# Twelve gate products ahead of every step of the grouped heads' attention, latent heads first, and one instruction less per row in the norms

## The chip, the cores and the metric

One core of a Trainium2 chip runs the whole kernel. The time is the device time of one launch, in microseconds (us). The engines are named as in the profile: PE (TensorE, matmuls; PEld its weight loads), DVE (VectorE), ACT (ScalarE), POOL (GpSimd) and SP, which issues the DMAs. Each has its own queue and works through it in order; they wait for one another through semaphores.

## The reference

Two transformer layers over 512 tokens of width 1024, then a second block with four more token mixers. The change touches the mixer of the two layers and all norms:

```
for l in range(2):
    x = x + 0.5 * g1 * swiglu(modulate(x, sh1, sc1), ...)
    x = x + g2 * token_mix(modulate(x, sh2, sc2), ...)
    x = x + 0.5 * g3 * swiglu(modulate(x, sh3, sc3), ...)

modulate(x, shift, scale) = rms_norm(x) * (1 + scale) + shift

token_mix(u):
    o_a = nsa_attention(...)   # grouped heads: 8 heads in 2 groups; compressed, selected and window branch
    o_b = mla_attention(...)   # latent heads: 8 heads, key width 64 + 32
    y = sigmoid(g_a) * (o_a @ w_branch_a) + sigmoid(g_b) * (o_b @ w_branch_b)
    return y @ w_out
```

`g_a` and `g_b` are `u` times the last 2048 columns of `w_in`: 16 groups of 128 columns. Softmax is masked and causal. With 512 tokens all blocks are selected, so the selected branch is a causal attention over all keys, like the window branch. Everything is fp32.

## The kernel before, in words

**Matmuls of weights.** Activations lie feature-major in SBUF, as 128 x 512 tiles `u[:, k, :]`. Each weight tile arrives by DMA in `raw` (512 KB for 8 blocks of 128 x 128), ACT rounds it to `wh` (L917), DVE writes the rest to `wl` (L1393). The activation is split in the same way into `uh` and `ul`. A block of k is then three products, `wh*uh`, `wl*uh`, `wh*ul` (helper `three`, L435 to L437), each with 512 columns. A list (`plan`) gives the order of the weight tiles. Every engine walks it with `get`, which prepares the tile two ahead.

**Norms.** DVE multiplies a row of x by the reciprocal root, which PE has spread into a PSUM bank (L1457). ACT scales and shifts the row (L951), ACT rounds it to `uh` (L953), DVE subtracts to get `ul` (L1427). The next matmul waits for the first `ul`. The order of the four is in `apply`, on ACT and on DVE.

**Attention of a layer** (`mix`, stages `m0` and `m1`). It is a software pipeline over 48 steps, each a pair of heads and one block i of 128 queries against 128(i+1) keys. 32 steps are grouped heads (kind `nsa`: 4 pairs, i from 0 to 3, two branches), then 16 latent heads (kind `mla`: 4 pairs, i from 0 to 3). A step t goes through

```
PE    scores(t)                        L638, two heads, banks 2*(t%2) and 2*(t%2)+1
DVE   add bias, row minimum (t)        L1660, 'soft' of both heads
ACT   exp (t)                          L1085
DVE   max, reciprocal, scale (t)       L1668, L1670, L1676 or L1678
PE    transpose (t)                    L544, 'turning', banks 4 and 5
ACT   copy (t)                         L1092
PE    values (t)                       L651, L657, banks 6 and 7
```

In each round of the loop PE issues scores(t), turning(t-2), values(t-3), in this order. DVE issues soft(t), then the scaling of t-1:

```
for t in range(len(pairs) + 1):        # DVE
    if t < len(pairs):  ... soft(t)
    if t > 0:           ... max, reciprocal, scale of t - 1
```

The grouped heads' soft needs `slope`, which POOL makes from the table `dist` (L2130) once the latent projections are done. The latent heads' soft needs the table `mask`.

**After the attention** come, for each m of 8, the gate group gA (24 products), the branch product wa (12), gB (24) and wb (12), L435 to L437; ACT takes the gate's tanh (L1110), DVE makes the sigmoid (L1691), the product with the branch (L1694), the sum (L1696) and the split `yh`, `yl`. Then eight groups `wo` read `yh`, `yl`.

Of the kernel before, what the change touches and what calls it, by code (L numbers as in the profile page):

```python
# [14 lines left out]
def plan():  # L15
# [42 lines left out]
    for l in range(2):  # L58
# [22 lines left out]
        for m in range(8):  # L81
            fm(f"gA{l}", 8, m)
            fm(f"wa{l}", 4, m)
            fm(f"gB{l}", 8, m)
            fm(f"wb{l}", 4, m)
# [141 lines left out]
def attention_pairs():  # L227


    u = [("nsa", hh, i, br) for hh in range(4) for i in range(4) for br in range(2)]  # L230
    return u + [("mla", j, i, 0) for j in range(4) for i in range(4)]


def program(nc, A, OUT):
# [42 lines left out]
    with ExitStack() as c:  # L277
        oA, oB = sb(c, "oA", [128, 4, 512]), sb(c, "oB", [128, 4, 512])
        with ExitStack() as c1:
# [6 lines left out]
            dist = sb(c1, "dist", [128, 512])  # L286
            mq = sb(c1, "mq", [128, 8, 512])
            mk = sb(c1, "mk", [128, 8, 512])
# [4 lines left out]
            with ExitStack() as c2:  # L293
                mmask = sb(c2, "mmask", [128, 512])
# [6 lines left out]
        yh, yl = sb(c, "yh", [128, 8, 512], F32R), sb(c, "yl", [128, 8, 512], F32R)  # L301
# [44 lines left out]

    ident, ones = col("ident", 0, 128), col("ones", 0, 128)
# [55 lines left out]
    def tensor_engine(pe, TE):  # L403
# [143 lines left out]
        def mix(l):  # L547
# [71 lines left out]
            pe.wait_ge(*s_act["kk", st])  # L619
            pe.wait_ge(*s_act["vt", st])  # L620
            pe.wait_ge(*s_act["pcT", st])
            for t in range(len(pairs) + 3):
                if t < len(pairs):
                    kind, h, i, br = pairs[t]
                    L = 128 * i + 128
                    if t == 32:
                        pe.wait_ge(*s_act["mk", st])
                        pe.wait_ge(*s_dve["mk", st])
                        pe.wait_ge(*s_dve["mq", st])
                        pe.wait_ge(*s_pool["mq", st])  # L630
                        pe.wait_ge(*s_act["mv", st])
                    o = [take(("S", (st, 2 * t + g)), 2 * (t % 2) + g) for g in range(2)]
                    for g in range(2):
                        if kind == "nsa":
                            q, k = oA[64 * g:64 * g + 64, h, sl(i)], kk[64 * g:64 * g + 64, br, 0:L]
                        else:
                            q, k = mq[0:96, 2 * h + g, sl(i)], mk[0:96, 2 * h + g, 0:L]
                        TE.matmul(o[g][:, 0:L], q, k, start=True, stop=True).then_inc(*s_pe.up(("ps", ("S", (st, 2 * t + g)))))  # L638
# [3 lines left out]
                if 0 <= t - 3 < len(pairs):  # L642
# [9 lines left out]
                    for j in range(i + 1):  # L652
                        for g in range(2):
# [4 lines left out]
                            if j == i:  # L658
                                last = g == 1 and i == 3 and (kind == "mla" or br == 1)
                                ins.then_inc(*s_pe.up(("pv", (st, n + g)), *([("ps", both)] if last else [])))  # L660
            s_pe.mark(("attend", st))
            ring[1] = 0
            for m in range(8):
                for x_, h_, l_ in (("A", oAh, oAl), ("B", oBh, oBl)):
                    fm(("g" + x_, st, m), f"g{x_}{l}", 8, m, uh, ul, ("u", st))
# [237 lines left out]
    def scalar_engine(act, SC):  # L903
# [41 lines left out]
        def apply(st, n, dst, scale, shift=None, before_k=None):  # L945
            for k in range(n):
                if before_k:
                    before_k(k)
                t0 = tmp[k % 4]
                act.wait_ge(*s_dve["ap", st, k])  # L950
                SC.activation(t0[:], t0[:], ACT.Identity, bias=0.0 if shift is None else shift(k), scale=scale(k)).then_inc(*s_act.up(("af", st, k)))  # L951
                act.wait_ge(*s_act.now())
                SC.activation(dst[:, k, :], t0[:], ACT.Copy).then_inc(*s_act.up(("uh", st, k)))  # L953
# [6 lines left out]
        def norm(st):  # L960
            q = MOD[st]
            apply(st, 8, uh, lambda k: mod[:, q + 8 + k:q + 9 + k], lambda k: mod[:, q + k:q + k + 1])
# [57 lines left out]
        def mix(l):  # L1020
# [38 lines left out]
            apply(("cq", st), 3, qh, lambda k: col(f"qn{l}", k))  # L1059
# [3 lines left out]
            for h in range(8):  # L1063
                fm(f"uq{l}", 3, h)
                copy(("uq", st, h), mq[0:64, h, :], bank(("uq", st, h))[0:64, :], ("mq", st, h), -(96.0 ** -0.5))
                if h == 4:
                    apply(("ckv", st), 2, ch, lambda k: col(f"kvn{l}", k))
# [10 lines left out]

            for t in range(len(pairs) + 3):
                if 0 <= t - 1 < len(pairs):  # L1080
                    L = 128 * pairs[t - 1][2] + 128
                    for n in (2 * t - 2, 2 * t - 1):
                        p = mP[n % 6]
                        act.wait_ge(*s_dve["s", (st, n)])
                        SC.activation(p[:, 0:L], p[:, 0:L], ACT.Exp, bias=two(n, 0), scale=-1.0, accum_out=two(n, 1)).then_inc(*s_act.up(("e", (st, n))))  # L1085
                if 0 <= t - 2 < len(pairs):
                    L = 128 * pairs[t - 2][2] + 128
                    for n in (2 * t - 4, 2 * t - 3):
# [3 lines left out]
                        SC.activation(mT[n % 4][:, 0:L], bank(("T", (st, n)))[:, 0:L], ACT.Copy).then_inc(*s_act.up(("pt", (st, n)), frees=("T", (st, n))))  # L1092
                if 0 <= t - 3 < len(pairs):
# [6 lines left out]
            for k in range(4):  # L1100
                for kind, o, h in (("nsa", oA, oAh), ("mla", oB, oBh)):
                    act.wait_ge(*s_act["o", st, kind, k])
                    SC.activation(h[:, k, :], o[:, k, :], ACT.Copy).then_inc(*s_act.up(("oh", st, kind, k)))
            for m in range(8):
                for b, (x_, w_) in enumerate((("gA", "wa"), ("gB", "wb"))):
                    fm(f"{x_}{l}", 8, m)
                    act.wait_ge(*s_pe["ps", (x_, st, m)])
                    if m > 1:
                        act.wait_ge(*s_dve["y", st, m - 2])
                    SC.activation(tmp[(2 * m + b) % 4][:], bank((x_, st, m))[:], ACT.Tanh, scale=0.5).then_inc(*s_act.up((x_, st, m), frees=(x_, st, m)))  # L1110
                    fm(f"{w_}{l}", 4, m)
                act.wait_ge(*s_dve["ysum", st, m])
                SC.activation(yh[:, m, :], tmp[2 * m % 4][:], ACT.Copy).then_inc(*s_act.up(("yh", st, m)))
# [250 lines left out]
        apply("f10", 8, uh, lambda k: mod[:, q0 + 8 + k:q0 + 9 + k], lambda k: mod[:, q0 + k:q0 + k + 1], rest)  # L1364
# [9 lines left out]
        apply("s", 8, uh, lambda k: small[:, 64 + k:65 + k])  # L1374
        copy(("r1",), acc[:], bank(("r1",))[:], "rowcopy")
        second()
        apply("up", 8, uh, lambda k: col("n2", k))
# [3 lines left out]
    def vector_engine(dve, V):  # L1381
# [67 lines left out]
        def apply(st, key, src, n, g, dst_h, dst_l, before_k=None, after_k=None):  # L1449
            for k in range(n + 1):  # L1450
                if k < n:
# [5 lines left out]
                    V.tensor_tensor(tmp[k % 4][:], src[:, k, :], more[:] if after_k and k else bank(g)[:], MUL).then_inc(  # L1457
                        *s_dve.up(("ap", st, k), frees=g if k == (0 if after_k else n - 1) else None))
                    if after_k:
                        after_k(k)  # L1460
                        low(dst_l[:, k, :], tmp[k % 4][:], dst_h[:, k, :], s_act["uh", st, k], (*key, k))
                elif after_k:
                    continue
                if k > 0 and not after_k:
                    low(dst_l[:, k - 1, :], tmp[(k - 1) % 4][:], dst_h[:, k - 1, :], s_act["uh", st, k - 1], (*key, k - 1))
# [61 lines left out]
        def mix(l):  # L1527
# [75 lines left out]
            apply(("cq", st), ("cq", st), cq, 3, ("rq", st), qh, ql)  # L1603
# [22 lines left out]
            for h in range(8):  # L1626
# [4 lines left out]
                if h == 4:  # L1631
                    dve.wait_ge(*s_dve["added", st, 4])
                    apply(("ckv", st), ("ckv", st), ckv, 2, ("rk", st), ch, cl)
# [7 lines left out]
            dve.wait_ge(*table(f"dist {st}"))  # L1641

            for t in range(len(pairs) + 1):
                if t < len(pairs):
# [37 lines left out]
            for k in range(4):  # L1682
                low(oAl[:, k, :], oA[:, k, :], oAh[:, k, :], s_act["oh", st, "nsa", k], ("oA", st, k))
# [747 lines left out]
```

## Time and profile before

| | |
|---|---|
| time, median of 3 runs | 3555.81 us (3555.67 to 3568.52) |
| time of the profiled execution | 3571.1 us |
| its span, first to last instruction | 3569.3 us |
| PE busy | 3455.7 us, 97% |
| DVE busy | 1800.9 us, 50% |
| ACT busy | 1237.3 us, 35% |
| mean granted TensorE clock | 0.975 of full speed |
| chain that ended last | PE 89%, DVE 6%, ACT 3% |

PE's matmuls are pipelined, and their ends are modelled: a 128x512 product is shown with 0.39 us, while the next one starts 0.23 us after it. For the cost of PE work, starts are to be read, not durations. An idle time shown in brackets is what is left after the modelled end.

### The profile page before, as it was taken

The page shows a single profiled execution, that of the slowest core. Times are in us where ns is not written, and L with a number is a line of the kernel's source. Part 1 is how long each engine was busy: PE and PEld are TensorE (multiplying, and loading weights), DVE is VectorE, ACT ScalarE, POOL GpSimd, SP SyncE. Part 2 cuts the span into 40 slices and gives each one's busy share as a digit, 9 for nine tenths or more (in the row PEclk, how much of TensorE's full clock was granted, in tenths as well). Part 3 has the DMA queues.
Part 4 walks back from the last instruction along what each step waited for, and adds up shares of the span by engine and source line. Part 5 has one row for each costly group of instructions (what it writes and reads, how often), then busy time and mean ns, then how long its engine had stood idle before and what let it go on. Part 6 is the DMA issues. An engine that isn't in the chain of part 4 may idle for free.

```text
span 3569.3 us, 40894 instructions
## 1 busy us (share of the span) xinstructions
PE 3455.7 (97%) x16646; PEld 2777.9 (78%) x16646; DVE 1800.9 (50%) x3132; ACT 1237.3 (35%) x2064; POOL 286.5 (8%) x238
## 2 busy tenths in 40 slices
PE   8999999999999999999899999999999999999999
PEld 6888776787888788877667878887778777878887
DVE  7666457645566733334674443334453665354433
ACT  4222337523222322223573232224322444124322
POOL 0000121002000200021200100012011000020000
PEclk9999999999999999999899999999999999899999
DMA  6565221133565533232102322322221223132332
GB/s 235 207 210 185 99 79 37 40 106 101 190 219 195 175 97 102 92 101 92 59 1 83 103 83 85 111 81 93 66 77 61 76 68 117 31 100 81 98 106 77
DMA packets 120217, 376.36 MB, mean 105 GB/s; under 512 B 13280, under 2 KB 28000, under 8 KB 120032
## 3 DMA queue, kind: packets, MB, share of 16 engines
q1 hardware_dynamic: 120032, 373.76, 32.2%
q8 instruction: 132, 2.16, 0.3%
q14 instruction: 53, 0.43, 0.0%
HBM read 371.61 MB, written 2.10 MB: 105 GB/s over the span
## 4 chain that ended last, share of the span: by engine, by line
PE 89%; DVE 6%; ACT 3%; issue 1%; POOL 1%; DMA 0%; SPq 0%; POOLq 0%; ACTq 0%; DVEq 0%
PE ps L435 25%; PE ps L436 25%; PE ps L437 25%; PE ps L638 2%; PE ps L544 2%; PE ps L657 1%; PE ps L478 1%; PE ps L485 1%; PE ps L469 1%; PE ps L471 1%; PE ps L470 1%; DVE s_wl L1393 1%; ACT s_wh L917 0%; ACT s_tmp L951 0%; POOL s_small L2061 0%
## 5 line engine op out<-in xcount | busy, mean ns | idle before, releaser
L1393 DVE TENSOR_TENSOR s_wl<-s_raw,s_wh 128x1024 fp32r<-128x1024 f32 (+3 forms) x645 | 708.3, 1100 | 867.3 <-ACT s_wh L917 865.2
L435 PE MATMUL ps<-s_uh,s_wh 128*128 128x512 f32 x2696 | 1075.1, 399 | 36.9 <-DVE s_ul L1427 23.9
L436 PE MATMUL ps<-s_uh,s_wl 128*128 128x512 f32 x2696 | 1060.0, 393 | 0.0
L437 PE MATMUL ps<-s_ul,s_wh 128*128 128x512 f32 x2696 | 1059.6, 393 | 0.0
L917 ACT ACTIVATE s_wh<-s_raw 128x1024 fp32r<-128x1024 f32 (+3 forms) x645 | 588.2, 913 | 742.1 <-PE ps L437 555.3
L435 PEld LDWEIGHTS ps<-s_uh,s_wh 128*128 128x128 f32 x2696 | 513.2, 190 | 155.5 <-issue 31.8
L436 PEld LDWEIGHTS ps<-s_uh,s_wl 128*128 128x128 f32 x2696 | 513.4, 190 | 107.9 <-issue 2.7
L437 PEld LDWEIGHTS ps<-s_ul,s_wh 128*128 128x128 f32 x2696 | 512.0, 190 | 108.7
L437 PE MATMUL ps<-s_fl,s_wh 128*128 128x512 f32 x960 | 378.2, 394 | 0.0
L435 PE MATMUL ps<-s_fh,s_wh 128*128 128x512 f32 x960 | 378.2, 394 | 0.0
L436 PE MATMUL ps<-s_fh,s_wl 128*128 128x512 f32 x960 | 378.2, 394 | 0.0
L984 ACT ACTIVATE s_fh<-s_tmp 128x512 fp32r<-128x512 f32 x120 | 75.8, 632 | 407.2 <-DVE s_tmp L1490 382.3
L436 PEld LDWEIGHTS ps<-s_fh,s_wl 128*128 128x128 f32 x960 | 179.5, 187 | 44.5
L437 PEld LDWEIGHTS ps<-s_fl,s_wh 128*128 128x128 f32 x960 | 179.5, 187 | 44.5
L435 PEld LDWEIGHTS ps<-s_fh,s_wh 128*128 128x128 f32 x960 | 179.5, 187 | 44.3
L978 ACT ACTIVATE s_tmp<-ps 128x512 f32<-128x512 f32 x120 | 71.7, 597 | 345.6 <-PE ps L437 343.2
L1402 DVE CUSTOM_DVE_ANT_0 s_raw<-s_raw,s_crow 128x1024 f32<-128x1024 f32 x144 | 181.3, 1259 | 0.8 <-DMA s_raw<-w 0.8
L2067 POOL TENSOR_TENSOR s_acc<-s_x 128x512 f32<-128x512 f32 x7 | 8.8, 1259 | 1776.4 <-DVE s_x L1472 1714.0
L1490 DVE TENSOR_TENSOR s_tmp<-s_tmp,ps 128x512 f32<-128x512 f32 x88 | 60.4, 687 | 171.7 <-PE ps L437 169.9
L1427 DVE TENSOR_TENSOR s_fl<-s_tmp,s_fh 128x512 fp32r<-128x512 f32 x120 | 83.1, 692 | 83.8 <-ACT s_fh L984 83.8
L1472 DVE SCALAR_TENSOR_TENSOR s_x<-ps,s_mod,s_x 128x512 f32<-128x512 f32 x80 | 60.0, 750 | 111.0 <-PE ps L437 111.0
L2072 POOL TENSOR_TENSOR s_acc<-s_acc,s_tmp 128x512 f32<-128x512 f32 x42 | 83.2, 1982 | 3.3
(405 smaller groups left out, 3673.4 us busy)
## 6 DMA issues: line engine op xcount, KB each, us to landing
s_raw<-w SPq DMA_DIRECT2D x616, 512.0 KB, 3.6
s_raw<-w SPq DMA_DIRECT2D x96, 192.0 KB, 2.4
s_raw<-w SPq DMA_DIRECT2D x64, 256.0 KB, 2.6
s_raw<-w SPq DMA_DIRECT2D x19, 128.0 KB, 2.1
s_x<-x SPq DMA_DIRECT2D x4, 512.0 KB, 6.2
out<-s_x SPq DMA_DIRECT2D x8, 256.0 KB, 2.2
s_raw<-w SPq DMA_DIRECT2D x4, 420.0 KB, 4.0
s_crow<-crow SPq DMA_DIRECT2D x2, 512.0 KB, 3.4
```

The source lines that it names most:

```text
L435: TE.matmul(o, w_hi(i, k), h, start=first, stop=False)
L436: TE.matmul(o, w_lo(i, k), h, start=False, stop=False)
L437: return TE.matmul(o, w_hi(i, k), l, start=False, stop=last)
L544: ins = TE.transpose(o[:, sl(j)], p[:, sl(j)], ident)
L638: TE.matmul(o[g][:, 0:L], q, k, start=True, stop=True).then_inc(*s_pe.up(("ps", ("S", (st, 2 * t + g)))))
L917: SC.activation(wh[slot[t]][:, 0:n], raw[t % NRAW][:, 0:n], ACT.Copy).then_inc(*s_hi.up(("hi", t)))
L978: SC.activation(s[:], bank(("g", st, jj))[:], ACT.Silu if u else ACT.Relu).then_inc(*s_act.up(("gate", st, jj), frees=("g", st, jj)))
L984: SC.activation(fh[:, j, :], s[:], ACT.Copy).then_inc(*s_act.up(("hh", st, jj)))
L1393: V.tensor_tensor(wl[w][:, 0:n], raw[t % NRAW][:, 0:n], wh[w][:, 0:n].bitcast(F32), SUB).then_inc(*s_lo.up(("lo", t)))
L1402: V.tensor_tensor_reduce(raw[i % NRAW][:], raw[i % NRAW][:], crow[:], 1.0, 0.0, MUL, ADD, mod[:, o:o + 1]).then_inc(*s_dve.up(("raw", i)))
L1427: V.tensor_tensor(dst, src, hi.bitcast(F32), SUB).then_inc(*s_dve.up(key))
L2072: PO.tensor_tensor(acc[:], acc[:], t[:], ADD).then_inc(*s_pool.up(("sq", st, m), ("sq", st)))
```

## The change

- The latent heads' 16 steps come first, the grouped heads' 32 after them.
- Of the 16 gate groups of a layer, 15 move into the grouped heads' steps: from the first of them (step 16) on, every step begins on PE with two quarters of a group, twelve products in one piece, for 30 steps. The groups use banks 2 and 3, and the grouped heads' scores only banks 0 and 1. The last group stands between the attention and wa.
- In all 48 steps PE now issues turning(t-2), values(t-3), and scores(t) last; before, scores(t) stood first. DVE's order is as it was.
- The tables `dist` and `mask` change places: `mask` is loaded early, `dist` once the latent projections are done.
- Gate tanhs go to `sA`, `sB` (the latent heads' `mq`, `mk`, by then read); `yh`, `yl` are now `uh`, `ul`. The sigmoid's scaling is folded into other instructions.
- Norms: DVE multiplies by the spread root and the scale in one instruction, ACT adds the shift and rounds in one, DVE adds the shift and subtracts in one: three instead of four.
- POOL clears its tiles in the mixer only when the norm is through.

```diff
 def attention_pairs():
-    u = [("nsa", hh, i, br) for hh in range(4) for i in range(4) for br in range(2)]
-    return u + [("mla", j, i, 0) for j in range(4) for i in range(4)]
+    u = [("mla", j, i, 0) for j in range(4) for i in range(4)]
+    return u + [("nsa", hh, i, br) for hh in range(4) for i in range(4) for br in range(2)]
+FIRST_NSA = 16
+FILLED = 15
+def gate_pieces(t):
+    return [(n // 4, n % 4) for n in (2 * (t - FIRST_NSA), 2 * (t - FIRST_NSA) + 1) if 0 <= n < 4 * FILLED]
...
+            def piece(n, quarter):
+                m, x_ = n // 2, "AB"[n % 2]
+                g = ("g" + x_, st, m)
+                if quarter == 0:
+                    gate_now["mix"] = get(f"g{x_}{l}", 0, 128 * m), take(g, 2 + n % 2)
+                i, o = gate_now["mix"]
+                for k in (2 * quarter, 2 * quarter + 1):
+                    ins = three(o[:, :], i, k, uh[:, k, :], ul[:, k, :], k == 0, k == 7)
...
             for t in range(len(pairs) + 3):
-                if t < len(pairs):
-                    ... scores(t)
+                for n in gate_pieces(t):
+                    piece(*n)
                 if 0 <= t - 2 < len(pairs):
                     for n in (2 * t - 4, 2 * t - 3):
                         turn((st, n), 4 + n % 2, mP[n % 6], 128 * pairs[t - 2][2] + 128)
                 if 0 <= t - 3 < len(pairs):
                     ... values(t - 3)
+                if t < len(pairs):
+                    ... scores(t)
             s_pe.mark(("attend", st))
+            for quarter in range(4):
+                piece(15, quarter)
...
-                SC.activation(t0[:], t0[:], ACT.Identity, bias=0.0 if shift is None else shift(k), scale=scale(k))
-                SC.activation(dst[:, k, :], t0[:], ACT.Copy)
+                if shift is None:
+                    SC.activation(dst[:, k, :], tmp[k % 4][:], ACT.Copy)
+                else:
+                    SC.activation(dst[:, k, :], tmp[k % 4][:], ACT.Identity, bias=shift(k), scale=1.0)
...
-                    V.tensor_tensor(tmp[k % 4][:], src[:, k, :], more[:] if after_k and k else bank(g)[:], MUL)
+                    V.scalar_tensor_tensor(tmp[k % 4][:], src[:, k, :], scale(k), more[:] if after_k and k else bank(g)[:], MUL, MUL)
...
+                    V.scalar_tensor_tensor(dst_l[:, k, :], tmp[k % 4][:], shift(k), dst_h[:, k, :].bitcast(F32), ADD, SUB)
```

**Where the latent heads' steps change.** PE's queue in the latent heads of layer 0, before; `s_mk,s_mq` are scores, `s_cst,s_mP` or `s_cst,s_tmp` turning, `s_mT,s_mv` values:

```order
L638 MATMUL ps2<-s_mk,s_mq 128x512
L638 MATMUL ps3<-s_mk,s_mq 128x512
L544 MATMUL ps4<-s_cst,s_mP2 128x128 x2
L544 MATMUL ps5<-s_cst,s_mP3 128x128 x2
L657 MATMUL ps7<-s_mT0,s_mv 64x128
L657 MATMUL ps7<-s_mT1,s_mv 64x128
L638 MATMUL ps0<-s_mk,s_mq 128x128
L638 MATMUL ps1<-s_mk,s_mq 128x128
L544 MATMUL ps4<-s_cst,s_tmp0 128x128 x3
L544 MATMUL ps5<-s_cst,s_tmp1 128x128 x3
```

and the same place with the change:

```order
L684 MATMUL ps0<-s_mk,s_mq 128x384
L684 MATMUL ps1<-s_mk,s_mq 128x384
L554 MATMUL ps4<-s_cst,s_tmp0 128x128 x2
L554 MATMUL ps5<-s_cst,s_tmp1 128x128 x2
L661 MATMUL ps7<-s_mT0,s_mv 64x128
L661 MATMUL ps7<-s_mT1,s_mv 64x128
L684 MATMUL ps2<-s_mk,s_mq 128x512
L684 MATMUL ps3<-s_mk,s_mq 128x512
L554 MATMUL ps4<-s_cst,s_mP0 128x128 x3
L554 MATMUL ps5<-s_cst,s_mP1 128x128 x3
```

The turning that followed scores(512 keys) turned two blocks, those of the step two before it; now it turns three blocks, those of the step just before the 512-key step. Between scores(t-1) and turning(t-2) there stood turning(t-3), values(t-4) and scores(t), and now nothing stands there.

**What DVE does between the two.** DVE's queue in the same steps with the change (`ISA` with `s_mmask` is the soft of one head, `s_mfew` alone its accumulator):

```order
L1707 ISA s_mP0,s_mfew<-ps2,s_mmask 128x512
L1707 ISA s_mfew 128x1
L1707 ISA s_mP1,s_mfew<-ps3,s_mmask 128x512
L1707 ISA s_mfew 128x1
L1715 TENSOR_SCALAR s_mfew<-s_mfew 128x2
L1717 RECIPROCAL s_mfew<-s_mfew 128x2
L1725 TENSOR_SCALAR s_tmp0<-s_tmp0,s_mfew 128x384
L1725 TENSOR_SCALAR s_tmp1<-s_tmp1,s_mfew 128x384
```

The scaling of the 384-key step, which its turning waits for, stands behind the soft of the 512-key step, which waits for that step's scores. This order is that of before.

**Where the grouped heads' steps change.** PE's queue in a step of the grouped heads with the change (`s_uh,s_wh` and so on are gate products, `s_kk,s_oA` scores, `s_mT,s_vt` values):

```order
L446 MATMUL ps2<-s_uh,s_wl0 128x512
L447 MATMUL ps2<-s_ul,s_wh0 128x512
L554 MATMUL ps4<-s_cst,s_mP0 128x128 x2
L554 MATMUL ps5<-s_cst,s_mP1 128x128 x2
L661 MATMUL ps6<-s_mT2,s_vt 64x128
L661 MATMUL ps6<-s_acc,s_vt 64x128
L684 MATMUL ps0<-s_kk,s_oA 128x384
L684 MATMUL ps1<-s_kk,s_oA 128x384
L445 MATMUL ps2<-s_uh,s_wh0 128x512
L446 MATMUL ps2<-s_uh,s_wl0 128x512
```

Here twelve gate products stand between scores(t-1) and turning(t-2), of which the first two and the last two are shown.

## Rows read from the trace of the kernel before

**Rows 1.** Busy time by stretch: PE, PEld, DVE, ACT, POOL, then clock, DMA, GB/s.

```profile
548.26:672.02 123.76, 117.38 (x977) 76.08 (x976) 94.00 (x384) 93.50 (x296) 12.22 (x8) 0.97 0.01 4
672.02:804.34 132.32, 132.32 (x578) 108.09 (x578) 60.80 (x84) 43.55 (x64) 0.00 (x0) 1.00 0.31 98
1759.10:1882.51 123.41, 116.94 (x972) 75.96 (x972) 94.06 (x384) 92.97 (x295) 11.68 (x8) 0.97 0.01 4
2770.00:2790.00 20.00, 16.72 (x79) 12.46 (x78) 13.84 (x50) 8.83 (x25) 0.00 (x0) 1.00 0.10 28
```

**Rows 2.** Timeline (start us, us, engine, line, op), the attention's first steps, layer 0.

```profile
549.01 0.49 PE L638 MATMUL ps<-s_kk,s_oA 64*128 64x128 f32 x4 [0.26 <-ACT s_mv L943]
550.11 0.29 DVE L1660 CUSTOM_DVE_ANT_0 s_mP<-ps,s_slope 128x128 f32<-128x128 f32 x1 [4.82 <-POOL s_slope L2130]
...
552.03 0.80 PE L638 MATMUL ps<-s_kk,s_oA 64*128 64x256 f32 x2 [2.52 <-DVE s_mfew L1660]
```

**Rows 3.** Timeline, four latent steps of layer 0, PE and DVE.

```profile
642.95 1.98 PE L638 MATMUL ps<-s_mk,s_mq 96*128 96x512 f32 x4
...
644.77 0.60 PE L544 MATMUL ps<-s_cst,s_mP 128*128 128x128 f32 x4
644.97 0.69 DVE L1660 CUSTOM_DVE_ANT_0 s_mP<-ps,s_mmask 128x512 f32<-128x512 f32 x1 [0.16 <-PE ps L638]
...
645.59 0.16 DVE L1668 TENSOR_SCALAR s_mfew<-s_mfew 128x2 f32<-128x2 f32 x1
...
645.99 0.75 DVE L1678 TENSOR_SCALAR s_tmp<-s_tmp,s_mfew 128x384 f32<-128x384 f32 x2
...
648.88 1.04 PE L544 MATMUL ps<-s_cst,s_mP 128*128 128x128 f32 x8
...
649.84 0.48 DVE L1678 TENSOR_SCALAR s_mP<-s_mP,s_mfew 128x128 f32<-128x128 f32 x2
...
653.39 0.70 PE L638 MATMUL ps<-s_mk,s_mq 96*128 96x512 f32 x1
```

**Rows 4.** Timeline, grouped heads, a turning that waits for its scaling.

```profile
596.13 0.73 DVE L1676 TENSOR_SCALAR s_mP<-s_mP,s_mfew,s_gt 128x256 f32<-128x256 f32 x2
...
596.69 0.41 PE L544 MATMUL ps<-s_cst,s_mP 128*128 128x128 f32 x2 [0.21 <-DVE s_mP L1676]
```

**Rows 5.** Timeline of PE, a piece of six gate products in the second block.

```profile
2777.70 0.50 PE L435 MATMUL ps<-s_uh,s_wh 128*128 128x512 f32 x1 [1.65 <-ACT s_sg L1143]
...
2779.20 0.59 PE L538 MATMUL ps<-s_xqk 128*128 128x256 f32 x2
```

**Rows 6.** Groups by line and shape: xcount | busy us, mean ns | idle before.

```profile
L917 ACT ACTIVATE s_wh<-s_raw 128x1024 fp32r<-128x1024 f32 x463 | 486.5, 1052 | 416.6 <-PE ps L437 258.2 <-DMA s_raw<-w 97.2 <-PE ps L471 60.3
L1393 DVE TENSOR_TENSOR s_wl<-s_raw,s_wh 128x1024 fp32r<-128x1024 f32 x463 | 596.4, 1290 | 573.6 <-ACT s_wh L917 573.3
L1472 DVE SCALAR_TENSOR_TENSOR s_x<-ps,s_mod,s_x 128x512 f32<-128x512 f32 x80 | 60.0, 750 | 111.0 <-PE ps L437 111.0
```

**Rows 7.** Timeline of PE, fifteen products that read uh, ul, and fifteen with yh, yl.

```profile
411.31 0.39 PE L435 MATMUL ps<-s_uh,s_wh 128*128 128x512 f32 x1
...
414.71 0.39 PE L435 MATMUL ps<-s_uh,s_wh 128*128 128x512 f32 x1
...
805.04 0.39 PE L435 MATMUL ps<-s_yh,s_wh 128*128 128x512 f32 x1
...
808.54 0.39 PE L435 MATMUL ps<-s_yh,s_wh 128*128 128x512 f32 x1
```

**Rows 8.** Timeline, first row of the norm ahead of the mixer, layer 0.

```profile
400.13 0.63 ACT L953 ACTIVATE s_uh<-s_tmp 128x512 fp32r<-128x512 f32 x1
...
400.79 0.69 DVE L1427 TENSOR_TENSOR s_ul<-s_tmp,s_uh 128x512 fp32r<-128x512 f32 x1 [1.03 <-ACT s_uh L953]
...
401.63 0.77 PE L435 MATMUL ps<-s_uh,s_wh 128*128 128x512 f32 x1 [3.19 <-DVE s_ul L1427]
```

More of the change, by code:

```diff
@@ L82, in plan @@
             fm(f"gA{l}", 8, m)
+            fm(f"gB{l}", 8, m)
+        for m in range(8):
             fm(f"wa{l}", 4, m)
-            fm(f"gB{l}", 8, m)
             fm(f"wb{l}", 4, m)
@@ L617, in mix @@
             s_pe.mark(("latent", st))
-            pe.wait_ge(*s_act["kk", st])
-            pe.wait_ge(*s_act["vt", st])
-            pe.wait_ge(*s_act["pcT", st])
-            for t in range(len(pairs) + 3):
-                if t < len(pairs):
[L624 to L638, printed above, removed]
+            def piece(n, quarter):
[6 more added lines that the diff above has]
+                    ins = three(o[:, :], i, k, uh[:, k, :], ul[:, k, :], k == 0, k == 7)
+                if quarter == 3:
+                    ins.then_inc(*s_pe.up(("w", i), ("ps", g)))
+            for t in range(len(pairs) + 3):
+                for n in gate_pieces(t):
+                    piece(*n)
                 if 0 <= t - 2 < len(pairs):
@@ L1077, in mix, with gate @@
             act.wait_ge(*s_pe["latent", st])
+            def gate(n):
+                m, x_ = n // 2, "AB"[n % 2]
+                act.wait_ge(*s_pe["ps", ("g" + x_, st, m)])
+                SC.activation((sA if n % 2 == 0 else sB)[:, m, :], bank(("g" + x_, st, m))[:], ACT.Tanh, scale=0.5).then_inc(
+                    *s_act.up(("g" + x_, st, m), frees=("g" + x_, st, m)))
             for t in range(len(pairs) + 3):
@@ L1085, in mix @@
                         SC.activation(p[:, 0:L], p[:, 0:L], ACT.Exp, bias=two(n, 0), scale=-1.0, accum_out=two(n, 1)).then_inc(*s_act.up(("e", (st, n))))
+                for n, quarter in gate_pieces(t):
+                    if quarter == 0:
+                        get(f"g{'AB'[n % 2]}{l}", 0, 128 * (n // 2))
                 if 0 <= t - 2 < len(pairs):
@@ L1092, in mix @@
                         SC.activation(mT[n % 4][:, 0:L], bank(("T", (st, n)))[:, 0:L], ACT.Copy).then_inc(*s_act.up(("pt", (st, n)), frees=("T", (st, n))))
+                for n, quarter in gate_pieces(t - 1):
+                    if quarter == 3:
+                        gate(n)
                 if 0 <= t - 3 < len(pairs):
@@ L1099, in mix @@
             act.wait_ge(*s_dve["attend", st])
-            for k in range(4):
-                for kind, o, h in (("nsa", oA, oAh), ("mla", oB, oBh)):
+            get(f"gB{l}", 0, 128 * 7)
+            for kind, o, h in (("nsa", oA, oAh), ("mla", oB, oBh)):
+                for k in range(4):
                     act.wait_ge(*s_act["o", st, kind, k])
                     SC.activation(h[:, k, :], o[:, k, :], ACT.Copy).then_inc(*s_act.up(("oh", st, kind, k)))
+            gate(15)
             for m in range(8):
[L1105 to L1111, printed above, removed]
+                fm(f"wa{l}", 4, m)
+                fm(f"wb{l}", 4, m)
                 act.wait_ge(*s_dve["ysum", st, m])
-                SC.activation(yh[:, m, :], tmp[2 * m % 4][:], ACT.Copy).then_inc(*s_act.up(("yh", st, m)))
+                SC.activation(yh[:, m, :], sA[:, m, :], ACT.Copy, scale=0.5).then_inc(*s_act.up(("yh", st, m)))
             for m in range(8):
@@ L1456, in apply @@
                         dve.wait_ge(*s_act["row", st])
-                    V.tensor_tensor(tmp[k % 4][:], src[:, k, :], more[:] if after_k and k else bank(g)[:], MUL).then_inc(
+                    V.scalar_tensor_tensor(tmp[k % 4][:], src[:, k, :], scale(k), more[:] if after_k and k else bank(g)[:], MUL, MUL).then_inc(
                         *s_dve.up(("ap", st, k), frees=g if k == (0 if after_k else n - 1) else None))
@@ L1640, in mix @@
             dve.wait_ge(*s_pe["latent", st])
-            dve.wait_ge(*table(f"dist {st}"))
             for t in range(len(pairs) + 1):
+                for n, quarter in gate_pieces(t):
+                    if quarter == 0:
+                        get(f"g{'AB'[n % 2]}{l}", 0, 128 * (n // 2))
                 if t < len(pairs):
@@ L2220, in sync_engine @@
             sp.wait_ge(*s_pe["latent", st])
-            tab(f"mask {st}", mmask[:], A["mask"])
+            tab(f"dist {st}", dist[:], A["dist"])
             if l == 0:
```

105 lines of the change are left out of this document (65 added, 40 removed).

## Prediction

> **What bounds the kernel now.** I read the stretches first, then the timeline inside them. In both layers' attention PE is busy 117 of 124 us, and in the gates and branches behind it 132.32 of 132.32 [rows 1]. DVE and ACT have 94 us each in an attention of 48 steps, under 2.0 us a step, while a step takes 2.6 us. So PE is the bound, and only two things can change the time: what PE waits for, and what a product costs it. Moving 15 gate groups saves no product. The most it can save is PE's waits in the attention: 123.76 less 117.38 is 6.4 us, and a clock of 0.97 means that some 3% of the stretch, 3.5 us, was lost at 1.2 GHz [rows 1]. That is 10 us a layer. As a record's modelled end hides a part of each gap, I take 12, and 10 to 14 as bounds. Where these are: at the start the first soft waits 4.82 us for POOL's slope, and PE then 2.52 us for a bank, and there the clock fell [rows 2]; the rest is spread in fractions of a microsecond. The gates' own stretch has nothing to save.
>
> **The new order, latent heads: the main term.** Turning(t-2) needs the scaling of t-2. On DVE that stands behind soft(t-1), which needs scores(t-1). Before, PE had turning(t-3), values(t-4) and scores(t) between scores(t-1) and turning(t-2), one whole step, 10.44 / 4 = 2.6 us from 642.95 to 653.39 [rows 3]. Now scores stand last in a round, and the latent steps have no piece at their head: nothing is between. PE stands still from the moment it could issue turning until DVE has gone through soft, max, reciprocal and one head's scaling. The length of that can be read off. With 512 keys PE is free at 644.77; DVE starts the second head's soft at 644.97, max at 645.59, scaling at 645.99, so 1.22 us after [rows 3]. From the start of a scaling to the turning that waits for it is 0.56 us [rows 4]. Together 1.8 us. For 256 keys the scaling starts 649.84 - 648.88 = 0.96 us after; its heads have 128 keys, 0.24 instead of 0.37 us each, so 0.43 behind it: 1.4 us [rows 3, 4]. The mean is 1.6 us. It is paid in steps 2 to 15, 14 times: 22.4 us a layer. Bounds: below, 1.0 us a step (if the transpose's start overlaps part of it), 14 us; above 2.0, 28 us. The exp, which the scaling needs too, was issued a step earlier and is long done.
>
> **The start.** The latent heads need no slope, so the 4.82 us wait of DVE goes and `dist` and POOL's work hide behind 16 steps. But their scores need all four copies of the latent values: the second pair of scores before had to wait for such a copy until 549.01 [rows 2], and the first had started at 548.26 [rows 1]. So the start slips by 0.8 us.
>
> **The grouped heads: pieces.** Twelve products stand ahead of every turning. A piece of six took 2779.20 - 2777.70 = 1.50 us [rows 5]. At the bare rate, fifteen in 3.40 us or 0.227 each [rows 7], six are 1.36, so a piece costs 0.14 us on top to get in and out of. Twelve: 2.72 + 0.14 = 2.86 us. 30 pieces: 4.2 us more than the same products in a row. What they give: the chain from scores to turning is, with the two heads' scores ending together and so both softs in series (0.6 more), at most 2.4 us, and the piece of 2.86 covers it; so the small waits there go (they are in the 12). What the pieces bring for the others is, in every second step, one 1024-wide rounding on ACT (1052 ns) and one rest on DVE (1290 ns) [rows 6], and a tanh: 2.8 us a step for ACT and 2.6 for DVE, where PE now takes 2.86 + 2.2 = 5.1. The weights are asked for more slowly than in the gates' stretch, where the DMA share was 0.31 [rows 1].
>
> **The end.** Two grouped steps, and the turning behind the last scores, have no piece: the bare chain three times, 2.0 to 2.4 us, 6.6; the drain of the last two turnings and values some 1.3, as before. 7.9 us. The last gate group covers the way from the last values to wa.
>
> **Sum of a layer:** 22.4 + 0.8 + 4.2 + 7.9 = 35.3 us of new waits and switches, less the 12 of before: +23.3. Two layers: +46.6 us. The split and sigmoid work behind has 5.6 us of PE per m and no new wait.
>
> **wo.** Fifteen products on `yh`, `yl` took 3.50 us, on `uh`, `ul` 3.40 [rows 7]. If that is due to where the tiles lie, the 384 products of wo gain 0.0067 us each, 2.6 us; if it is not, nothing. I take 2.
>
> **Norms.** The first row's chain goes straight to PE: the wait for the first `ul` is 3.19 us [rows 8]. The subtraction could start when the second ACT instruction does now: 400.79 - 400.13 = 0.66 us sooner. Its two DVE instructions with a scalar take 750 ns [rows 6] instead of 0.69, 0.12 lost: 0.53 net, eight norms, 4.2 us. The inner norms of the mixer (cq, ckv) are partly covered; I take 1 us a layer. Together 6; bounds 2 and 10.
>
> **Clock.** The old start's fall goes with its wait (it is in the 12). The new latent steps leave PE still for 1.6 of each 4.2 us. In 2770 to 2790 PE stood still for 3.3 of 20 us, once for 1.65 at a stretch, and the clock stayed at 2.4 GHz [rows 1, 5]; at the attention's start it fell to 1.2 after 2.52 us [rows 2]. The new waits lie between, nearer to the first. I expect a fall now and then, +3 us in all. All latent steps at 1.2 GHz is a rival.
>
> The Trainium skill, "TensorE: Matmul & The Clock Gate", Part 4: PE-mode transpose, says that transposes don't count as busy for the clock as other matmuls do. By that rule the latent steps, a quarter of which are transposes, would look idler than their records, and the first rival below would be the forecast. The trace of before does not bear it out: its attention has as many transposes and after the start keeps the full clock, though there with hardly a wait beside them.
>
> **Total:** +46.6 - 2 - 6 + 3 = +42 us on the profiled execution's 3571.1: 3613. That execution stands 15.3 us over the median of the three runs, 3555.8, which I take to be luck unconnected with the change. So the forecast for the median is **3598 us**, 1.2% slower. A measurement of this kernel can tell about 0.5%, 18 us, from no change.
>
> **Rivals.**
> - *Clock low through the latent heads.* For it: waits in every one of 14 steps. Against: the full clock in 2770 to 2790. About three quarters of the 10.44 us per four steps is columns, which double: +7.8, four times, +31 us a layer if it is low all the time, so 3598 + 62 = 3660; low half the time 3629. Chance 0.16.
> - *The filled steps are not PE's.* ACT's rounding stands behind its exps, DVE's rest behind that, and the next soft behind the rest: soft 1.3, exps 1.4, rounding 1.05, rest 1.3 add up to 5.0 us, as long as PE's 5.1. Should POOL's slopes or a late weight stretch it, each of 15 new tiles holds PE up by some 0.5 us: +15 in both layers, 3613. Chance 0.10.
> - *Not slower.* It decides from the point at which DVE has the scaling of t-2 done before scores(t-1) ends, so that PE finds it ready in the latent steps. Against: DVE's order has the soft first, before and now. For: only that the trace of before hardly shows the wait, as a step covered it. Then the 22.4 and most of the 6.6 are gone: 35.3 - 22.4 - 5 = 8 against 12, so -4 a layer, -8 in both, -2 - 6 for wo and norms: 3540. Chance 0.12.
> - The forecast's own case: 0.62.
>
> **How the numbers follow.** In its own case the sum moves with the wait per step (14 to 28 us a layer around 22.4, so -17 to +11 for both), the 12 (4 down), the norms and wo (4 either way) and the clock (up to 10): 3575 to 3625. To hold 8 in 10 the range takes in the second rival and half of the first: 3572 to 3642. Faster by over 0.5% is a part of the last rival, 0.04; within 0.5% the rest of it and the lower edge of my own case, 0.09; slower 0.87.
>
> **What would show it.** In the latent steps of the changed kernel, the first transposes of each step with an idle time of 1 to 1.5 us (the modelled end hides some) put down to DVE's scaling L1725, and a step of 4.2 us instead of 2.6. The grouped steps at 5.0 to 5.2 us with next to no idle time. A stretch from the first scores to the end of the last gate group of some 234 us at full clock. No wait of DVE for the slope. wo's products at 0.227. The norm's first product 0.5 us sooner. I am wrong if the latent steps stay under 3 us, or if idle time appears ahead of the gate products.

## The result, and the profile after

| | before | changed |
|---|---|---|
| time, median of 4 launches each | 3559.7 us (3555.7 to 3568.5) | 3631.2 us (3616.6 to 3643.0) |
| ratio | | 1.0193, 95% interval 1.0172 to 1.0214 |
| profiled execution | 3571.1 us | 3616.6 us, span 3614.7 us |
| PE busy | 3455.7 us | 3467.0 us, 96% |

The change makes the kernel 1.9% slower. The forecast was 3598 us, in 3572 to 3642. The table has four launches of before, one more than the table ahead of the prediction. The profiled execution is the fastest of the changed kernel's four, 3616.6 us with a mean granted clock of 0.973; the others, 3624.9, 3637.5 and 3643.0 us, had 0.970, 0.965 and 0.963. The four of before stand within 13 us of each other, these within 26.

The stretches of the changed kernel, from its trace (columns as in [rows 1]): latent heads of layer 0, grouped heads of layer 0 with their pieces, latent heads of layer 1, and in layer 0 the last gate group with the branch products.

```profile
543.88:614.14 70.26, 50.79 (x254) 30.51 (x255) 28.16 (x118) 31.08 (x92) 5.97 (x4) 0.77 0.02 5
614.14:786.06 171.92, 165.27 (x1084) 120.54 (x1083) 84.94 (x281) 90.33 (x234) 6.15 (x4) 0.97 0.12 38
1784.49:1850.11 65.62, 46.04 (x253) 27.47 (x254) 28.10 (x117) 30.84 (x91) 5.96 (x4) 0.84 0.02 6
786.06:836.12 50.06, 50.06 (x216) 40.25 (x216) 34.97 (x54) 20.28 (x34) 0.00 (x0) 1.00 0.36 105
```

Before, the grouped and the latent steps of layer 0, each from their first scores to their last:

```profile
548.26:621.82 73.56, 68.82 (x586) 42.14 (x586) 59.11 (x243) 56.68 (x183) 12.22 (x8) 0.95 0.02 5
624.17:665.23 41.06, 40.55 (x312) 28.20 (x311) 29.23 (x123) 30.22 (x97) 0.00 (x0) 1.00 0.00 1
```

The sixteen latent steps are where the time went. Before, they took 41 us. Now they take 70 and 66 us, PE is idle for 19.5 of each, and the clock is at 0.77 and 0.84 of full speed, so half of the first stretch and a third of the second ran at 1.2 GHz. In the stretch of the pieces PE is busy for 165.27 of 171.92 us; the 6.7 us in which it waits are ahead of the three turnings that have no piece, 2.0 to 2.4 us each.

The same place as [rows 3], four latent steps at full clock, PE and then DVE, start us, us, engine, line, operation, and in brackets the idle time:

```profile
568.58 1.56 PE L684 MATMUL ps<-s_mk,s_mq 96*128 96x384 f32 x4
571.55 0.68 PE L554 MATMUL ps<-s_cst,s_tmp 128*128 128x128 f32 x4 [1.42 <-ACT s_mP L1116]
572.16 0.44 PE L661 MATMUL ps<-s_mT,s_mv 128*64 128x128 f32 x4
572.53 1.98 PE L684 MATMUL ps<-s_mk,s_mq 96*128 96x512 f32 x4
576.13 0.85 PE L554 MATMUL ps<-s_cst,s_mP 128*128 128x128 f32 x6 [1.62 <-ACT s_mP L1116]
...
577.50 0.71 PE L684 MATMUL ps<-s_mk,s_mq 96*128 96x128 f32 x4
579.50 1.07 PE L554 MATMUL ps<-s_cst,s_mP 128*128 128x128 f32 x8 [1.28 <-DVE s_mP L1725]
...
581.30 1.13 PE L684 MATMUL ps<-s_mk,s_mq 96*128 96x256 f32 x4
583.65 0.50 PE L554 MATMUL ps<-s_cst,s_tmp 128*128 128x128 f32 x2 [1.22 <-ACT s_mP L1116]
...
585.10 1.24 PE L684 MATMUL ps<-s_mk,s_mq 96*128 96x384 f32 x3
```

DVE's rows in the second of these steps:

```profile
573.69 0.69 DVE L1707 CUSTOM_DVE_ANT_0 s_mP<-ps,s_mmask 128x512 f32<-128x512 f32 x1 [2.02 <-PE ps L684]
...
574.55 0.69 DVE L1707 CUSTOM_DVE_ANT_0 s_mP<-ps,s_mmask 128x512 f32<-128x512 f32 x1 [0.16 <-PE ps L684]
...
575.17 0.16 DVE L1715 TENSOR_SCALAR s_mfew<-s_mfew 128x2 f32<-128x2 f32 x1
...
575.57 0.75 DVE L1725 TENSOR_SCALAR s_mP<-s_mP,s_mfew 128x384 f32<-128x384 f32 x2
```

Four steps take 585.10 - 568.58 = 16.5 us, 4.1 each instead of 2.6. The 512-key scores, with the 1.82 us of [rows 3], leave PE free at 574.35; the transposes start at 576.13, 1.78 us later. In between DVE runs through the second head's soft (574.55), the max (575.17) and the scaling (575.57), and the transposes follow the scaling's start by 0.56 us. Three of the four brackets name ACT's exp, but by these starts it is DVE's scaling, L1725, that the transposes follow. The releaser is inferred; the neighbours' start times decide, and in the code `turn` waits, beside its bank, for `s_dve["p", g]`, the scaling, alone.

The two ends of a piece of twelve, to be held against [rows 5]:

```profile
620.10 0.50 PE L445 MATMUL ps<-s_uh,s_wh 128*128 128x512 f32 x1
...
622.96 1.04 PE L554 MATMUL ps<-s_cst,s_mP 128*128 128x128 f32 x8
```

It takes 2.86 us, and no turning behind a piece waits. From the scores of the first grouped step, at 619.68, to those of the thirtieth, at 764.70, there are 29 steps with a piece, 5.00 us each.

### The profile page after: what moved, and what is told of

Its sections match the earlier page's. It is cut to its first block, busy times and chain, and to the rows that moved or that the text cites. A ratio compares the mean times of both kernels' runs of the same rounds, so it can differ in the third digit from the quotient of the medians.

```text
span 3614.7 us, 40747 instructions
## 1 busy us (share of the span) xinstructions
PE 3467.0 (96%) x16646; PEld 2778.2 (77%) x16646; DVE 1792.3 (50%) x3100; ACT 1198.3 (33%) x1990; POOL 287.3 (8%) x238
## 4 chain that ended last, share of the span: by engine, by line
PE 91%; DVE 4%; ACT 3%; issue 1%; POOL 1%; DMA 0%; SPq 0%; POOLq 0%; ACTq 0%; DVEq 0%
PE ps L445 26%; PE ps L447 25%; PE ps L446 25%; PE ps L684 3%; PE ps L554 2%; PE ps L661 2%; PE ps L488 1%; PE ps L495 1%; PE ps L479 1%; PE ps L481 1%; PE ps L480 1%; DVE s_wl L1427 1%; ACT s_mP L1116 1%; ACT s_wh L942 0%; POOL s_small L2107 0%
## 5 line engine op out<-in xcount | busy, mean ns | idle before, releaser
L445 PE MATMUL ps<-s_uh,s_wh 128*128 128x512 f32 x2824 | 1132.3, 401 | 32.4 <-DVE s_ul L1489 12.8
L446 PE MATMUL ps<-s_uh,s_wl 128*128 128x512 f32 x2824 | 1110.5, 393 | 0.0
L447 PE MATMUL ps<-s_ul,s_wh 128*128 128x512 f32 x2824 | 1110.0, 393 | 0.0
L445 PEld LDWEIGHTS ps<-s_uh,s_wh 128*128 128x128 f32 x2824 | 537.7, 190 | 178.5 <-issue 49.9
L447 PEld LDWEIGHTS ps<-s_ul,s_wh 128*128 128x128 f32 x2824 | 536.5, 190 | 114.4
L446 PEld LDWEIGHTS ps<-s_uh,s_wl 128*128 128x128 f32 x2824 | 537.5, 190 | 111.7 <-issue 2.8
L1116 ACT ACTIVATE s_mP<-s_mP,s_mfew 128x256 f32<-128x256 f32 (+3 forms) x128 | 70.7, 553 | 84.9 <-DVE s_mfew L1707 84.8
```

The source lines that it names most:

```text
L445: TE.matmul(o, w_hi(i, k), h, start=first, stop=False)
L446: TE.matmul(o, w_lo(i, k), h, start=False, stop=False)
L447: return TE.matmul(o, w_hi(i, k), l, start=False, stop=last)
```

## The experiments

The theory: PE's order in the latent steps costs some 45 us by itself, and the clock that falls there costs what the time has over my sum. Rivals: the pieces and the end of the attention are the cost; the clock costs nothing; the order costs little. Ratios are to launches of the kernel before on the same chip, whose medians were 3564.2, 3563.9 and 3564.5 us in the three sets.

### Scores first again in the latent steps

```diff
             for t in range(len(pairs) + 3):
+                if t < FIRST_NSA: ... scores(t)
                 for n in gate_pieces(t): piece(*n)
                 ... turning(t - 2), values(t - 3)
-                if t < len(pairs): ... scores(t)
+                if FIRST_NSA <= t < len(pairs): ... scores(t)
```

> The changed kernel with one thing put back: in the 16 latent steps scores(t) stand first in the round again, the grouped steps keep their twelve products and scores last. Order theory (the prediction's): the bare chain of 1.6 us in 14 latent steps goes, and with it the falls of the clock there, so a latent step is back at 2.6 us and the stretch from the first scores to the first gate product at 42 us instead of 70 and 66 us. The time falls from 3631 by 45 for waits and some 15 to 20 for the clock, to 3565, 3555 to 3580. Rival theory (the pieces and the end of the attention are the cost): the time stays above 3610.

Measured: 3559.8 us, ratio 0.9993 (0.9984 to 1.0002), 12 launches, of which one stood far out at 4915.4, with a mean granted clock of 0.649; why isn't known. Latent and grouped steps of both layers:

```profile
547.09:587.55 40.46, 38.63 (x245) 25.96 (x246) 28.36 (x117) 27.03 (x88) 5.97 (x4) 0.92 0.04 11
593.07:749.73 156.66, 152.36 (x994) 111.05 (x992) 78.22 (x262) 83.30 (x220) 6.15 (x4) 0.99 0.13 41
1757.67:1794.98 37.31, 35.54 (x245) 23.69 (x246) 28.30 (x117) 26.91 (x88) 5.96 (x4) 1.00 0.05 15
1800.51:1955.71 155.20, 150.90 (x993) 110.11 (x992) 78.23 (x262) 83.21 (x220) 6.15 (x4) 1.00 0.14 42
```

This one edit, with all pieces left in, takes away 71 us: the whole loss. From the first scores to the last the latent steps take 40 and 37 us instead of the 70.0 and 65.6 of the changed kernel. That is 58 us, nearly all of the 59 that lie between the two profiled executions; the changed kernel's is its fastest. The rival, that the pieces and the end are what makes the change a loss, falls.

### Work in the wait: products, then transposes

Four products of 512 columns (`spare` is 4 in the first of a latent step's two turnings) write a bank that the transposes overwrite; then eight transposes stand in their place.

```diff
         def turn(g, b, p, L, spare=0):
             o = take(("T", g), b)
+            for _ in range(spare):
+                TE.matmul(o[:, :], uh[:, 0, 0:128], uh[:, 0, :], start=True, stop=True)
             pe.wait_ge(*s_dve["p", g])
```

> The changed kernel with four more fp32r products of 512 columns (0.91 us) in every latent step, put into PE's wait ahead of the transposes. They write a bank that the transposes then overwrite and that nobody reads, so nothing is computed differently. Clock theory: the wait of 1.6 us a step stays as long as it was, but PE's clock no longer falls to 1.2 GHz in the latent steps; from the first scores to the first gate product there are 59 to 61 us in both layers instead of 70 and 66, and the time is 3600, 3590 to 3612, with less spread between launches. Rival theory (the falls cost next to nothing, the waits are all of it): 3631 within 8. Second rival (the products delay the transposes): longer, up to 16 times 2 times 0.9, 3660.

```diff
-            for _ in range(spare):
-                TE.matmul(o[:, :], uh[:, 0, 0:128], uh[:, 0, :], start=True, stop=True)
+            for j in range(2 * spare):
+                TE.transpose(o[:, sl(j % 4)], ident, ident)
```

> As the run with four products in PE's wait, with eight transposes of 128 columns in their place (0.108 us apart in the trace of before, so 0.87 us instead of 0.91). Nothing reads what they write. Theory that any work counts for the clock: as with the products, no fall in the latent steps, 3600, 3590 to 3610. Theory of the Trainium skill, TensorE: Matmul & The Clock Gate, that a transpose does not count as other matmuls do: the clock falls in the latent steps as in the changed kernel, stretches of 66 to 72 us, 3631, 3615 to 3645.

Measured: 3599.5 us with the products (3597.8 to 3599.7, ratio 1.0104, 1.009 to 1.0118), 3600.6 us with the transposes (3599.0 to 3601.8, ratio 1.0098, 1.0081 to 1.0115). The latent steps with products, layers 0 and 1:

```profile
543.99:603.30 59.31, 53.32 (x310) 33.75 (x310) 28.74 (x118) 30.81 (x92) 5.96 (x4) 1.00 0.02 6
1775.23:1833.61 58.38, 52.76 (x309) 33.76 (x310) 27.90 (x117) 30.75 (x91) 5.97 (x4) 1.00 0.03 9
```

and with transposes:

```profile
545.02:603.30 58.28, 52.05 (x365) 36.45 (x366) 27.82 (x117) 30.75 (x91) 5.96 (x4) 1.00 0.03 8
1774.16:1833.59 59.43, 53.64 (x366) 37.41 (x366) 28.06 (x117) 30.75 (x91) 5.96 (x4) 0.97 0.03 9
```

PE does 56 more products a layer (x310 against x254), and the kernel is 32 us faster than the changed one. The clock is at 1.00 where it was at 0.77 and 0.84, and the spread between launches shrinks from 26 us to 2. The wait itself is still there. PE with the products in it, a step of 512 keys:

```profile
568.39 1.98 PE L686 MATMUL ps<-s_mk,s_mq 96*128 96x512 f32 x4
569.81 1.48 PE L553 MATMUL ps<-s_uh 128*128 128x512 f32 x4
...
571.90 0.94 PE L556 MATMUL ps<-s_cst,s_mP 128*128 128x128 f32 x6 [0.62 <-DVE s_mP L1727]
```

From the scores to their transposes there are 3.51 us, against 3.60 in the changed kernel, and here the bracket names the scaling too. So the two costs are apart: 3631.2 - 3599.5 = 32 us is the clock, 3599.5 - 3559.8 = 40 us is the wait. The ratios, 1.0193, 1.0104 and 0.9993, give the same 32 and 40. With transposes the clock fell once, for 3.4 us in layer 1, and the time is 1 us longer: they hold the clock nearly as well as products do. The Trainium skill, "TensorE: Matmul & The Clock Gate", Part 4: PE-mode transpose, says beside its figures for a bf16 transpose that they don't count as busy in the same way; here, with fp32 transposes beside fp32 matmuls, the measurement differs from it.

### Scores last alone, in the kernel before

```diff
             for t in range(len(pairs) + 3):
-                if t < len(pairs): ... scores(t)
                 ... turning(t - 2), values(t - 3)
+                if t < len(pairs): ... scores(t)
```

> The kernel before with PE's order alone changed: scores(t) last in each round, in all 48 steps; grouped heads first, no gate products, norms as before. Order theory: the bare chain stands in every step, 14 times 1.6 us in the latent and some 32 times 2.0 to 2.4 us in the grouped heads, 92 us a layer at full clock, so 3560 + 180 = 3740, and up to 3820 with the clock at 1.2 GHz for most of it. Rival (the order costs little, the pieces and the latent-first order did): under 3600.

Measured: 3835.9 us, ratio 1.0764 (1.0738 to 1.079). Its grouped and its latent steps, layer 0:

```profile
548.64:717.24 168.60, 109.95 (x607) 66.56 (x608) 60.06 (x244) 64.21 (x188) 12.22 (x8) 0.63 0.01 2
723.27:795.89 72.62, 51.91 (x300) 32.39 (x298) 29.02 (x121) 32.68 (x94) 0.00 (x0) 0.83 0.00 1
```

The grouped steps, 73.6 us before (548.26 to 621.82), take 168.6 when nothing covers the chain, three quarters of it at 1.2 GHz. So the twelve products do cover it in the changed kernel. The time is 16 us over the upper end of what was expected.

### Without pieces

Scores first everywhere on four banks, all sixteen gate groups after the attention; latent heads first, three-instruction norms and `yh`, `yl` in `uh`, `ul` stay.

```diff
-FILLED = 15
+FILLED = 0
...
-            for quarter in range(4):
-                piece(15, quarter)
+            for n in range(FILLED, 16):
+                for quarter in range(4):
+                    piece(n, quarter)
```

> The changed kernel without pieces: scores first in all 48 steps, on four banks as before, and all sixteen gate groups after the attention, ahead of the branch products. What stays of the change: latent heads first, three instructions per row in the norms, yh and yl in uh and ul. Piece theory (the prediction's terms): against the run with the latent scores first (3560), 30 switches of 0.14 us and two or three bare chains at the end go, 4.2 + 6.6 us a layer, and some 4 us a layer of small waits in the grouped steps come back: 14 us less, 3546; the kernel before less 6 to 11 for the norms, 5 for the last matrix and 2 times 5 to 8 for the start without the slope gives 3540 by the other way. So 3535 to 3550. Rival (the pieces pay, since they cover waits that the earlier order leaves): 3560 or more.

Measured: 3543.6 us, ratio 0.9941 (0.9926 to 0.9956). Latent steps, grouped steps, and the way to the end of the gates, layer 0:

```profile
544.78:582.16 37.38, 35.55 (x246) 23.69 (x247) 28.38 (x117) 26.92 (x88) 5.97 (x4) 1.00 0.04 11
583.49:656.23 72.74, 70.28 (x638) 44.34 (x636) 61.14 (x251) 59.68 (x192) 6.14 (x4) 1.00 0.01 2
656.23:751.32 95.09, 94.57 (x474) 78.00 (x471) 27.79 (x38) 33.34 (x54) 0.00 (x0) 1.00 0.23 70
```

So the pieces, in the better of the two orders tried, cost 16 us: 3559.8 against 3543.6. A filled step takes 5.00 us, in the run with latent scores first as in the changed kernel. The same 29 steps here, from the scores at 583.49 to those at 650.79, take 2.32 us each. The 2.68 between them is not more than the twelve products, 12 * 0.227 = 2.72: the small waits of an unfilled step and the 0.14 us of a piece cancel. The 16 us have to lie at the entry and the end. At the end three turnings without a piece wait 2.0 to 2.4 us each, 6.7 us a layer, where here the last turnings wait 0.5.

### Norms alone, and POOL's clearing alone

The norms' three instructions in the kernel before, as in the diff of the change; then, in the kernel before, nothing but this wait:

```diff
             st = f"m{l}"
+            pool.wait_ge(*s_dve["u", st, 7])
             PO.memset(kc[:], 0.0)
```

> The kernel before with the norms in three instructions per row and nothing else of the change. Prediction's sum: 0.53 us for each of eight norms and 1 us a layer for the inner ones, 6 us less, so 3550 to 3556 beside 3560; after each norm the first product stands 0.5 us sooner (first gap of 11.02 us between the last product of the first feed-forward and the first product of the mixer down to 10.5). By what the changed kernel's trace showed (that gap 9.66 and 9.12 us, the mixer's projections 2.4 us shorter) it could be more: 12 to 15 us less, 3546. Rival: what was seen there comes from other parts of the change (POOL's later clearing): nothing here, 3560.

> The kernel before with one wait more: POOL clears its tiles in the mixer only when the norm is through, as in the change. In before the four instructions of DVE that spread the root (128 columns, L1431) take 1.99 us beside POOL's clearing, in the changed kernel 0.88 without it. If POOL's clearing is the cause: 0.88 us here too, and the way from the last product of the feed-forward to the first of the mixer 11.02 less 0.7, 10.3 us. If the norm's other instructions are the cause: 1.99 and 11.02 as before. The time changes by too little to be seen, 1 to 2 us.

Measured: norms 3553.3 us, ratio 0.9974 (0.9965 to 0.9983), so 6 to 12 us less. The way from the last product of the feed-forward to the first of the mixer is 10.39 us in both layers, against 11.02. With the clearing later it is 10.09 and 9.69. DVE's spreading of the root in layer 0 of before, from the timeline:

```profile
395.24 1.99 DVE L1431 TENSOR_SCALAR s_tmp<-s_cst,s_small 128x128 f32<-128x128 f32 x4 [1.23 <-POOL s_small L2061]
```

and in the run with the clearing later:

```profile
395.92 0.88 DVE L1431 TENSOR_SCALAR s_tmp<-s_cst,s_small 128x128 f32<-128x128 f32 x4 [1.23 <-POOL s_small L2061]
```

The same four instructions take 1.99 us beside POOL's clearing and 0.88 without. The one execution with the clearing later, 3561.9 us, says nothing of the time.

### 64 bytes

Products on `uh` and `ul` start every 0.227 us, on other split tiles every 0.233 [rows 7]. In a partition `uh` and `ul` lie 32 bytes past a multiple of 128, the others 96. So, in the kernel before, one unused tile:

```diff
     small = sb(top, "small", [128, 96])
+    sb(top, "pad", [128, 16])
```

> The kernel before with an unused tile of 64 bytes per partition ahead of fh, and nothing else: every tile behind it lies 64 bytes higher. The products of 512 columns on uh and ul start every 0.227 us, those on fh, fl, bh, bl, oAh, oAl, oBh, oBl, yh and yl every 0.233 us; uh and ul lie at 32 bytes past a multiple of 128 in a partition, the others at 96. Place theory: the others' pitch falls to 0.227 as well; some 3850 products by 0.0063 us are 24 us, so 3536, 3530 to 3542. Rival (the pitch goes with the tile or with what the stage does, not with the place): 3560, no change.

Measured: 3537.7 us, ratio 0.9929 (0.9912 to 0.9945). Fifteen products on `fh` and `fl`, from the first's start to the sixteenth's, in the timeline of before:

```profile
147.94 0.39 PE L435 MATMUL ps<-s_fh,s_wh 128*128 128x512 f32 x1
...
151.44 0.39 PE L435 MATMUL ps<-s_fh,s_wh 128*128 128x512 f32 x1
```

and with the 64 bytes:

```profile
148.37 0.39 PE L436 MATMUL ps<-s_fh,s_wh 128*128 128x512 f32 x1
...
151.77 0.39 PE L436 MATMUL ps<-s_fh,s_wh 128*128 128x512 f32 x1
```

Fifteen take 3.40 us instead of 3.50, and the same holds for `oAh`, `bh` and `yh`. It is the place.

The same in the kernel without pieces, and then with 24 unused floats more ahead of `x`:

> The kernel without pieces and with the 64 bytes. Both theories add: 3546 less 3450 products by 0.0063 us (the last matrix has its gain already), 22 us: 3524, and faster than both kernels by 1%. Rival: as without the 64 bytes, 3546.

> As the one before, with 96 more unused bytes ahead of x, so that x, the weights, uh, ul and nearly all other tiles lie at a multiple of 128 bytes. If the pitch of a product depends on the place within 128 bytes alone and 32 is as good as 0: 3524, no change to the run before. If a place at a multiple of 128 is better by as much as 32 is better than 96 (0.0063 us a product, some 12000 products): 75 us less, 3450. If it is worse by that: 3600.

Measured: 3517.4 us, ratio 0.9871 (0.9853 to 0.9889), 7 us less than was expected and the fastest of all, 1.3% faster than the kernel before and 3.1% faster than the changed one. At a multiple of 128: 3525.0 us, ratio 0.9888 (0.9871 to 0.9906), with the same pitch of 0.227 us. So 0 and 32 are alike for the pitch. In the profiled execution the clock fell in the latent steps of both layers here and of one layer there, and such a fall makes that stretch 3.2 us longer (40.5 against 37.3 us); whether falls make all of the 8 us, or the place of another engine's tile, wasn't tried.

## Why the prediction was right, and what in it was wrong

**The sign and its cause: right.** Putting scores back alone gives back 71 of 71.5 us, and nothing else in the change is a loss of that kind.

**"14 times 1.6 us": right.** Waits of 1.78 us for 512 keys and 1.38 for 256 (from 581.30 plus the 0.97 us that these scores take in the run with the scores first, to 583.65) against 1.8 and 1.4. At full clock, which the run with products shows, the latent steps take 59.3 and 58.4 us. In the time it is 40 us for both layers, where 44.8 was written.

**"Clock, +3 us in all": the step that failed.** It measured 32 us by the medians. I had weighed the waits against two places of before, one wait of 1.65 us that kept 2.4 GHz and one of 2.52 us that lost it, and taken a wait of 1.6 to 1.8 as near the first. The second was misread. PE stands still there from 549.50 to 552.03 us, and the clock was down before 551.5, when the wait had lasted under 2 us, not much longer than the longest of the new ones:

```profile
551.10:551.30 0.20, 0.00 (x0) 0.00 (x0) 0.00 (x0) 0.00 (x0) 0.20 (x1) 1.00 0.00 0
551.50:551.70 0.20, 0.00 (x0) 0.00 (x0) 0.12 (x1) 0.00 (x0) 0.12 (x2) 0.50 0.00 0
```

The comparison also left out that the first stood alone in 20 us and these come every 4 us. But that alone doesn't bring the clock down. In layer 1 of the changed kernel the same waits, in steps of the same length, kept 2.4 GHz for 42 us:

```profile
1808.20:1850.10 41.90, 28.18 (x189) 17.05 (x188) 19.07 (x81) 21.53 (x63) 0.00 (x0) 1.00 0.00 1
```

What decides it from one stretch to the next stays open. The profiled execution shows half clock in the latent steps for 31.5 us in layer 0 and 20.5 in layer 1. Its time is 17 us above that of the profiled execution with the products; what is left of the 32 us of the medians is in the slower launches, whose clocks are lower and which have no profile. The rival "clock low through the latent heads", at half the time 3629, describes what happened; it had 0.16. With its 31 us in place of the 3, everything else as written, the forecast would have been 3626. The time is within the stated range only because half of this rival was taken into it: my own case was given 3575 to 3625, and 3631.2 is outside.

**"The pieces": right in size.** A piece took 2.86 us as worked out, a filled step 5.00 where 5.0 to 5.2 was written, no turning behind a piece waits, and the three bare chains at the end wait 6.7 us where 6.6 was written. The rival that ACT and DVE bound these steps falls. From the first scores to the end of the last gate group, 234 us were forecast at full clock. With the products in the wait it is 781.29 - 543.99 = 237.3 and 2010.17 - 1775.23 = 234.9; in the changed kernel it is 247.7 and 242.8.

**wo: right.** The placement is the cause, and here the kernel had much more to give: my term counted the 384 products of wo, while ten times as many start 0.0067 us late.

**Norms: low.** 6 us were written, 6 to 12 measured. The first row gave 0.63 instead of 0.53. Of the inner norms I had taken 1 us a layer; the stretch from the mixer's first product to the first scores is 1.2 and 3.1 us shorter in the run with norms alone, and in each layer a part of that is a fall of the clock that before had and that run had not (534 to 538 and 1742 to 1746 us of before).

**Left out: POOL's later clearing.** The diff names it and the sum has no term for it. It gives 0.9 and 1.3 us in that one profile, since the clearing had slowed DVE on the path. The Trainium skill, "SBUF — State Buffer", "Who interferes with whom", says that VectorE in its two-port modes and GpSimd block each other; the 1.99 and 0.88 us agree, though the trace doesn't say which mode the instruction ran in.

**The whole sum.** By the medians, in steps: from the kernel before to the one without pieces (norms, clearing, start, place of `yh`) -20; the pieces and the end +16; the order in the latent steps +40; the clock +32; together +67, to 3631.2. Mine, cut in the same way: norms and wo -8, the old waits -24, pieces and end +24, start +1.6, together -6 where the first two measured -4; the order +45 for 40; the clock +3 for 32. (Against the set of launches with which the result was taken, +67 reads +71.5, since before stood at 3559.7 there and at 3564 here.)

## What to carry to other kernels

Put work between a matmul and the instruction that needs its softmax in every step, not only in those for which filling is at hand: here fourteen waits a layer cost more than everything else gave. A short wait in every step can be paid twice, once for itself (40 us here) and once for the clock (32 us); a single wait of the same length elsewhere in the trace was no guide to the second. A pipeline whose engine is already busy for 95% of the time leaves little to fill: the pieces cost 16 us even in the better order. Moving tiles by 64 bytes saved 26 us.

## What the runs showed of the hardware

- 128x512 fp32r products start every 0.227 us when the moving tile lies 0 or 32 bytes past a multiple of 128 in its partition, and every 0.233 us at 96. Over this kernel it is 26 us. In the run with the 64 bytes the weight tiles stayed where they were, so it is the moving tile's place. Other places weren't tried.
- Waits of 1.4 to 1.8 us in steps of 4.1 us bring TensorE down to 1.2 GHz in some stretches and not in others, and differently from launch to launch: 26 us of spread, 2 to 3 us once the waits are filled.
- Filling a wait with work that nobody reads made the kernel 32 us faster, with eight transposes as with four products.
- Four TENSOR_SCALAR of 128 columns on DVE take 0.88 us, and 1.99 us beside POOL's MEMSETs, which only write.
